# A two-layer hybrid trunk on one core: what of the modulation is made ahead of the first norm, and where the rest is made

## The reference, cut to what matters

```python
mod_l = (silu(c)     @ ada_w[i] + ada_b[i])   # 6 x 1024: shift, scale, gate of the mixer; shift, scale, gate of the MoE
mod_c = (silu(c_ctx) @ ada_w[i] + ada_b[i])
h = rmsnorm(x, ng[0]) * (1 + mod[1]) + mod[0]          # ahead of the mixer
x = x + mod[2] * rmsnorm(mixer(h), ng[1])
h = rmsnorm(x, ng[2]) * (1 + mod[4]) + mod[3]          # ahead of the MoE
x = x + mod[5] * rmsnorm(moe(h), ng[3])
```

## Time and profile before

| | us |
|---|---|
| median of three runs | 2848.91 |
| profiled execution | 2851.62 |
| its span, first to last instruction | 2849.9 |
| constants and modulation, up to the last column copy | 0 to 52.7 |
| first norm | 54.1 to 68.6 |
| projection with the other 24 pieces | 68.9 to 436.7 |
| PE busy over the span | 2375.7 (83%) |
| DVE, ACT, POOL busy | 800.5, 525.7, 323.1 |

### The profile page before, as it was taken

One profiled execution on the slowest core, in us unless ns is written; L12 is line 12 of the kernel. 1 busy time (PEld: TensorE's weight loads), 2 busy tenths in 40 slices (PEclk: granted clock), 3 DMA queues, 4 the chain that ended last, 5 costly groups with the idle time before them and its releaser, 6 DMA issues. The chain is left out here.

```text
span 2849.9 us, 41403 instructions
## 1 busy us (share of the span) xinstructions
PE 2375.7 (83%) x18056; PEld 1190.5 (42%) x18056; DVE 800.5 (28%) x1636; ACT 525.7 (18%) x1106; POOL 323.1 (11%) x483
## 2 busy tenths in 40 slices
PE   4999998479789888888959968999986988788887
PEld 1333445354344333333324446888873322222222
DVE  2002617380231111111143025676632110101001
ACT  1000212770210000000030024444411000000001
POOL 0000000350100000000032006353410000000000
PEclk8999999689899999999979978999988999999999
DMA  7765210212299999999942234223226999999997
GB/s 275 251 237 193 71 52 30 71 51 96 81 404 425 425 424 424 425 425 424 425 163 66 69 136 75 53 48 69 40 51 258 424 425 425 425 424 425 425 425 294
DMA packets 203348, 707.61 MB, mean 248 GB/s; under 512 B 90404, under 2 KB 125964, under 8 KB 149280
## 3 DMA queue, kind: packets, MB, share of 16 engines
q1 hardware_dynamic: 202240, 704.57, 63.0%
q10 hardware_dynamic: 928, 0.39, 0.1%
HBM read 688.68 MB, written 16.20 MB: 247 GB/s over the span
## 5 line engine op out<-in xcount | busy, mean ns | idle before, releaser
L1593 PE MATMUL bank<-moe_w,moe_xT 128*32 128x512 f32 (+3 forms) x2760 | 576.3, 568 | 148.8 <-DMA moe_w<-in_exp_w 148.2
L1593 PEld LDWEIGHTS bank<-moe_w,moe_xT 128*32 128x32 f32 (+1 forms) x2760 | 177.1, 123 | 546.7 <-issue 371.2
L1620 PE MATMUL bank<-moe_w,moe_hidT 128*32 128x512 f32 (+1 forms) x1276 | 294.4, 594 | 14.4 <-ACT moe_hidT L1661 10.2
L1691 DVE TENSOR_TENSOR moe_silu<-bank,moe_silu 64x512 f32<-64x512 f32 (+3 forms) x96 | 61.8, 644 | 709.1 <-ACT moe_silu L1654 709.1
L1654 ACT ACTIVATE moe_silu<-bank 64x512 f32<-64x512 f32 (+3 forms) x96 | 53.1, 554 | 998.4 <-PE bank L1593 998.4
L1620 PEld LDWEIGHTS bank<-moe_w,moe_hidT 128*32 128x32 f32 (+1 forms) x1276 | 94.7, 122 | 189.6 <-issue 174.3
L1735 POOL TENSOR_TENSOR moe_xn<-moe_xn,moe_w 128x1024 f32<-128x1024 f32 x6 | 18.1, 3016 | 1351.9 <-ACT moe_w L1670 1351.9
L1704 DVE COPY moe_rows<-bank 32x512 f32<-32x512 f32 x96 | 65.8, 686 | 372.0 <-PE bank L1620 371.1
L467 PE MATMUL bank<-w_slab,mixT 128*128 128x512 f32 x384 | 166.4, 593 | 1.5 <-PE bank L467 1.5
L1855 PE MATMUL bank<-mixture,rw_slab 128*128 128x512 f32 (+1 forms) x384 | 143.6, 527 | 4.6 <-PE bank L1855 3.7
L464 PE MATMUL bank<-mixT,w_slab 128*128 128x512 f32 x320 | 142.6, 599 | 1.7 <-PEq L292 1.7
(11 more groups left out here) (486 smaller groups left out, 3076.4 us busy)
## 6 DMA issues: line engine op xcount, KB each, us to landing
moe_w<-in_exp_w SPq DMA_DIRECT2D x346, 1408.0 KB, 28.8
x_res<-in_exp_w SPq DMA_DIRECT2D x38, 1408.0 KB, 25.1
conv_out<-in_ada_w SPq DMA_DIRECT2D x24, 1536.0 KB, 6.4
w_slab<-in_ab_w_in SPq DMA_DIRECT2D x11, 2048.0 KB, 9.1
ada_slab<-in_ada_w SPq DMA_DIRECT2D x8, 1536.0 KB, 12.5
mixT<-ss_rows SPq DMA_DIRECT2D x32, 256.0 KB, 3.2
wo_slab<-in_ab_w_out SPq DMA_DIRECT2D x16, 512.0 KB, 3.5
x_inv_and_t<-x_blocks SPq DMA_DIRECT2D x32, 256.0 KB
```

What stands on the lines that cost most here:

```text
L1593: mm = pe.matmul(g.ps[k][64 * m:64 * m + M, 0:hi - lo], xg[:, i % 2, j, c, :], w[:, (2 * m + r) * FF + lo:(2 * m + r) * FF + hi], start=(c ...
L1620: mm = pe.matmul(g.ps[5 + m][64 * m:64 * m + M, :], hidt[:, c, :], w[:, at:at + 512], start=(c == 0), stop=(c == FC - 1))
L1691: ins = dve.tensor_tensor(hid[:, lo:hi], g.ps[k][64:64 + M, 0:hi - lo], hid[:, lo:hi], ALU.mult)
```

## The change

- `stage_constants_and_modulation` and the first `stage_norm` become one stage, `stage_start`. It loads the tokens first and then only columns 0 to 2047 of layer 0's `ada_w` (shift and scale of the first norm), in eight pieces of 1 MB through five buffers. The parameter tables are loaded from ACT's queue, ahead of ACT's first activation.
- The norm writes `g.hT` without modulation. PE's order is: two token tiles, piece 0, tile 2, piece 1, tile 3, piece 2, the tables, pieces 3 to 7.
- `c_cols` is padded to 32 columns for each slice, and a piece is four products of 32 x 512 into four column groups of one bank (`ada_product`). One copy and four transposes then give the columns on the chip (`shift_and_scale`); the way through DRAM is gone.
- In `stage_project` DVE and ACT first multiply and shift `g.hT` in place, eight operations of 128x256 each (`modulated`), and the matmuls of step 0 wait for them slice by slice.
- The other ten vectors are five groups of eight pieces of 1 MB, 40 pieces in all, through three buffers behind steps 0 to 26. Their bias and gain rows are loaded by SP ahead of a group's first piece (`params_in`); for group 0 and 1 SP first waits until DVE has filled the rows (`s_fill`), for groups 3 and 4 until the rows of groups 0 and 1 are stored. Layer 1's shift and scale (group 2) are turned on the chip behind step 18.
- A weight slab is loaded in two halves, each with a semaphore of its own.

Cut to its core:

```diff
+def ada_product(g, pe, ps, dc, piece):
+    for j in range(4):
+        mm = pe.matmul(ps[32 * j:32 * j + 32, :], g.ccol[:, dc, :], piece[:, 512 * j:512 * j + 512], start=(dc == 0), stop=(dc == DC - 1))
+    return mm
...
+def stage_start(g, sq):
...
+                sp.dma_start(g.x[:, 0:2, :], a["ctx"].rearrange("b (t p) d -> p (b t) d", p=P)).then_inc(s_x[0], 16)
+                sp.dma_start(g.x[:, 2:4, :], a["x"].rearrange("b (t p) d -> p (b t) d", p=P)).then_inc(s_x[1], 16)
                 for dc in range(DC):
...
+                    if dc >= RING:
+                        sp.wait_ge(s_used, dc - RING + 1)
+                    sp.dma_start(slots[dc % RING], a["ada_w"][0, dc * P:(dc + 1) * P, 0:MODW]).then_inc(s_ada[dc % RING], 16)
+                g.slab_in(sp, 0, COL_Q)
+                g.slab_in(sp, 1, COL_K)
...
+                turn(0)
+                turn(1)
                 pe.wait_ge(s_silu, 1)
...
+                piece(0)
+                turn(2)
+                piece(1)
+                turn(3)
+                piece(2)
+                pe.wait_ge(s_par, 16 * 16)
...
+                for dc in range(3, DC):
+                    piece(dc)
+                pe.wait_ge(s_evict, 1)
+                pe.wait_ge(s_eva, NT)
...
+        GROUPS = ((0, 2), (0, 4), (1, 0), (1, 2), (1, 4))
+        BUFFER = (0, 1, None, 0, 1)
+        PIECES = len(GROUPS) * DC
+        LAST = 27
         AFTER = {}
-        for p in range(3 * DC):
-            AFTER.setdefault(p - p // 5 if p < 20 else p - 4, []).append(p)
+        for p in range(PIECES):
+            AFTER.setdefault(p * LAST // PIECES, []).append(p)
...
+                    gi, dc = divmod(p, DC)
+                    layer, k = GROUPS[gi]
+                    if dc == 0 and BUFFER[gi] is not None:
+                        params_in(gi)
...
+                    if gi < 2:
+                        sp.wait_ge(s_fill, 1)
+                    else:
+                        sp.wait_ge(s_rowout, 2 * 64)
...
+                            if n == 0 and m == 0:
+                                pe.wait_ge((s_modv, s_moda)[dc % 2], 2 * (dc // 2 + 1))
...
+            def modulated(op, odd, done):
+                for dc in range(odd, DC, 2):
+                    for st in range(2):
+                        part = g.hT[:, dc, (1 - st) * SEG:(2 - st) * SEG]
+                        shift, scale = (g.cols[:, c:c + 1] for c in (mod_col(0, st, 0, dc), mod_col(0, st, 1, dc)))
+                        op(part, part, scale, shift).then_inc(done, 1)
...
-        stage_constants_and_modulation(g)
         layer0(g)
```

More of the change, by code:

```diff
@@ new lines, in shift_and_scale @@
+def shift_and_scale(g, dve, layer, ps, done):
+    view = ps[:, :].rearrange("p (b j r) -> p j b r", b=4, r=32)
+    at = lambda c0, k: g.cols[:, c0 + 8 * k:c0 + 8 * k + 8].rearrange("p (j b) -> p j b", j=2)
+    bias = COL_BIAS[layer]
+    for st in range(2):
+        c0 = COL_MOD[layer] + 16 * st
+        g.dve.do(dve.tensor_tensor(at(c0, 0), view[:, 0:2, :, st], at(bias, 0), ALU.add))
+        g.dve.do(dve.scalar_tensor_tensor(at(c0, 1), view[:, 2:4, :, st], 1.0, at(bias, 1), ALU.add, ALU.add))
+    g.dve.join(dve)
+    for st in range(2):
+        c0 = COL_MOD[layer] + 16 * st
+        g.dve.do(dve.tensor_tensor(at(c0, 1), at(c0, 1), at(bias, 2), ALU.mult))
+    g.dve.join(dve)
+    dve.memset(g.small[:, 0:1], 0.0).then_inc(done, 1)
@@ L173, in _ @@
[L173 to L177, removed]
@@ new lines, in _, with turn @@
+                pe.wait_ge(s_load, 32)
+                pe.transpose(g.ps[1][:, 0:16], crow[:, :], g.ident[0:16, 0:16]).then_inc(s_tr, 1)
+                def turn(t):
+                    pe.wait_ge(s_xn, t + 1)
+                    if t >= 3:
+                        pe.wait_ge(s_eva, t - 2)
+                        pe.wait_ge(s_evd, t - 2)
+                    for h in range(2):
+                        for i in range(4):
+                            mm = pe.transpose(g.ps[2 + 2 * (t % 3) + h][:, i * P:(i + 1) * P], g.xn[:, t, (4 * h + i) * P:(4 * h + i + 1) * P], g.ident[:, :])
+                        mm.then_inc(s_tp, 1)
@@ L282, in stage_norm @@
+                for dc in range(3, DC):
+                    piece(dc)
+                pe.wait_ge(s_evict, 1)
+                pe.wait_ge(s_eva, NT)
+                for b in range(4):
+                    mm = pe.transpose(g.ps[2][:, b * P:(b + 1) * P], mrow[:, b * P:(b + 1) * P], g.ident[:, :])
+                mm.then_inc(s_mt, 1)
 def stage_norm(g, layer, which, t0, ctx, sq=None, begin=None):
@@ L394, in _ @@
                         g.slab_in(sp, n, c0)
[L395 to L402 removed]
                     if n == 1:
+                        for p in range(ARING):
+                            ada_in(p)
                         sp.wait_ge(s_spread, 1)
```

389 lines of the change are left out of this document (164 added, 225 removed).

## The result

| | before | after |
|---|---|---|
| median of the runs, us | 2850.70 (4 runs, 2847.16 to 2852.69) | 2826.30 (4 runs, 2824.16 to 2829.26) |
| profiled execution, its span | 2851.62, 2849.9 | 2826.01, 2824.3 |
| step 0 of the projection begins | 68.93 | 35.81 |
| first product of the mLSTM begins | 437.72 | 412.01 |
| from there to the end | 2412.2 | 2412.3 |

The account below looks back on a forecast made before the run. The serial start up to 68.93 us, then PE in the projection, bound the kernel. Terms -33.9 - 4.5 + 6.4 + 2.0 + 3.0 + 0.7 = -26.3 gave 2825.3 profiled, 2822.6 us as median; range 2811 to 2835.

Parts of the forecast that it names:

- step 0 begins: Projection's first step moves from 68.93 to 35.0 us, a gain of 33.9; bounds 33 and 41.
- pieces and visits on PE: Projection: 40 pieces at 0.86 and 27 visits at 0.3 replace 24 at 1.71 and 20 at 0.3; gain 4.5 us.
- step 0 at a low clock: First projection step at half clock, by the skill page: about 1.7 us, mentioned but left out of the sum.
- waits at pieces 0 and 1: Behind step 0, PE waits 4.8 us for piece 0's load and 1.6 more for piece 1.
- slow records behind them: After the wait at piece 0, a lowered PE clock costs 2.0 us, bounds 0 and 4.
- waits at pieces 24 and 25: Parameter rows must wait until group 1 is stored behind step 15: 1.4 us at piece 24, 1.6 at piece 25.
- transposes behind step 18: Projection: the four transposes there cost PE 0.7 us.
- The ring: Start: the last piece needs piece 2's buffer, free at 24 to 26 us, so it lands at 29.3 to 31.
- The rival by which less of the start is gained: ACT's issues cost 0.80 each, step 0 begins at 41 us with slow records; 2830 us, chance 0.20.
- Four groups side by side: Each piece's four products run at once, 0.86 us a piece; if not, 1.72 and 2860 us, chance 0.07.
- Costs of nothing: DVE's row work and the later convolution stay hidden, some 20 us of cover remaining; piece 3 hidden with 2.6 to spare.

Follow-up runs that it names:

- version with idle products: Changed kernel plus unread TensorE products behind pieces 5 to 7, behind the four transposes and ahead of step 0; median 2825.59 us.
- the earlier store: Changed kernel with the rows of group 1 stored behind step 13 instead of step 15; median 2820.99 us.
- the version with two edits: Changed kernel with the first three projection pieces loaded in stage_start and group 1's rows stored two steps sooner; median 2814.82 us, 0.9863 of before.
- the version with the fourth product twice: Changed kernel in which each piece makes its fourth product a second time in the same quarter of PSUM; median 2859.51 us.

## Why the prediction was right, and where it was not

The forecast held, and in the main its mechanism. 2826.3 lies 3.7 us above 2822.6; 1.8 of it is that the median of before rose from 2848.91 to 2850.70 with a fourth run. By its own terms, from the trace of after:

| term | predicted | measured | from |
|---|---|---|---|
| step 0 begins | -33.9 | -33.1 | 35.81 against 68.93 |
| pieces and visits on PE | -4.5 | -4.3 | 13 visits of 2.0 and 14 of 1.13, against 16 of 1.96 and 4 of 3.67 before; a step without pieces is 27.70 / 4 |
| step 0 at a low clock | not in the sum | +2.9 | 10.00 against 7.10 |
| waits at pieces 0 and 1 | +6.4 | +3.1 | 2.20 + 0.92 |
| slow records behind them | +2.0 | +2.8 | 0.5 and 0.9 in the pieces, 1.46 in step 1 |
| waits at pieces 24 and 25 | +3.0 | +2.2 | 0.84 + 1.31 |
| transposes behind step 18 | +0.7 | +0.5 | 223.93 to 224.42 |
| sum | -26.3 | -25.9 | marker: -25.7 |

That the sum is so near is partly luck: the start and the slow records came 0.8 dearer each, the waits at pieces 24 and 25 0.8 cheaper.

- **The start.** The first square was forecast at 8.8 and came at 9.15, the last piece at 29.3 to 31 and came at 30.54, step 0 at 35.0 and came at 35.81. That transfers come last is shown by the waits of 1.41 and 1.43 there. The ring, from which the 29.3 to 31 was worked out, did not set it: piece 2 was used at 21.68 and not at 24 to 26, since the later tiles were turned in 1.09 and not 1.9, and the last piece, issued by 23.13, landed 7.4 us later and not some 5, behind what was queued at 402 GB/s. The two misses offset each other, so that the number for the last piece was right by luck. The rival by which less of the start is gained fell: ACT's issues took 0.40 each, not 0.80.
- **The step that failed: the sum takes step 0 at full speed.** I worked out the clock only behind the wait of piece 0. The sentence on the Trainium skill (TensorE: Matmul & The Clock Gate, Why this matters for your kernels) pointed there: idle gaps between bursts of products leave the next burst slow. The trace agrees, with 0.50 in 36 to 38 us behind a light stretch (PE busy 5.14 of 10 us, then 0.19 of 2); the cost was 2.9 where that sentence gave 1.7. Its other half, that transposes do not count as work for the clock in the same way (the Trainium skill, TensorE: Matmul & The Clock Gate, Part 4), the traces do not bear out. The prediction read 0.50 at 64 to 66 us of before as agreement and stopped one window short:

```profile
66.00:68.00 2.00, 1.21 (x7) 0.90 (x5) 1.33 (x5) 1.51 (x4) 0.00 (x0) 0.75 0.25 92
68.00:70.00 2.00, 1.07 (x3) 0.62 (x4) 1.52 (x6) 0.00 (x0) 1.11 (x3) 1.00 0.43 74
```

From 58.91 us on PE had made nothing but transposes, and the clock was up before step 0, which took 7.10.

- **Why it did not show in the sum.** The load of piece 0 was forecast to land 12 us behind the beginning of step 0, issued at +7.3; it was issued at +7.1 and landed at +12.2. Piece 1 was forecast 2.5 us behind and came 2.45 behind. These times were right; what was wrong is when PE is there: at +10.0, not +7.2. So 2.9 moved from the wait into the step. The version with idle products shows the other side: with step 0 in 7.03, the wait is 4.79, and the prediction said 4.8. The two errors cancel by construction, since one event, the landing of the load, ends both: PE can't go on before it, whether it spends the time in step 0 or waiting.
- **Waits at pieces 24 and 25** had the cause that was named (the earlier store takes them away) and were a little dear: the six parameter loads take 1.8 us on SP (41.15 to 42.91), not the 2.6 that the earlier trace rows gave.
- **Four groups side by side.** A piece takes 0.86 as taken; the Trainium skill (TensorEngine Tiling (Array Packing), Available Configurations) lists 128x32 as four tiles, and this trace agrees. The 0.43 a round of the prediction is 1.71 / 4; the row it names gives 1.89 / 4, 0.47. Nothing in the sum hangs on it.
- **Costs of nothing** held: the convolution's cover was 27 us where some 20 were forecast, piece 3 was issued 22.2 us behind the beginning of step 0 (57.98) where 23.0 were forecast, and not waited for (PE waits for a load at pieces 0, 1, 24 and 25 alone), and no change of length behind the marker can be told from the spread of single executions.
- **Spread.** The other 1.3 us between -25.7 and the medians' -24.4 is within what runs of one kernel differ by (5 us here).

## What to carry to other kernels

Where a load ends a wait, what is gained ahead of it on the waiting engine only makes the wait longer: first ask what the queue issues ahead of the load. (With the waits at pieces 0 and 1 gone, the idle products that make step 0 faster still moved the marker by 0.6 us at most in the executions here.) Six parameter rows of a few KB, put with their wait for DVE ahead of 1 MB pieces that PE needs at once, cost some 5 us, and a store two steps too late 2; both were to be had by moving issues alone. And when an order on PE names small tables between large pieces, the tables' queue decides: on ACT's PE did not wait for them, behind the pieces on SP's it waited 4.29 us and step 0 began 1.7 later.

## What the runs showed of the hardware that was not expected

- The granted clock fell in a light stretch and not only in a stop: in the version with two edits it is 0.68 in 32 to 34 us, with PE busy for 0.95 of 2.00, and 1.00 again from 40 us. When it falls differs between versions whose programs are alike there (34 to 36 in the change), so step 0 took 8.5 to 10.0 us without any edit to it, and where no wait stands behind step 0 the marker carries that much chance.
- The length of a wait alone does not say whether the clock falls: behind 2.20 us of idle PE in the change the next window has 0.62, while behind 3.29 us in the version with the fourth product twice pieces 0 and 1 and step 1 ran at full speed. What tells the two apart stays open.
- An issue on SP can take long: the first two gathers held SP for 5.32 us (44.30 to 49.62) while three pieces of 1 MB were moving, the next two, of the same size, for 1.21. With the pieces issued earlier they took 3.17, while the second weight slab was moving. That what is queued is the reason is likely, and not tested.
- Transposes alone were followed by a rise of the clock, in the kernel before (0.75 in 66 to 68 us, 1.00 in 68 to 70) and by their times also in the change: there the first sixteen took 3.68 us, as sixteen did at 0.50 before, piece 0 behind them ran in 1.11, and eight between pieces took 1.09 from 18.63 on. The windows print 1.00 for the first sixteen as well, which their times contradict: ahead of about 18 us the column of the clock does not tell the clock.
